# Gate products woven between attention steps in pieces of two blocks, with branches placed anew

## The chip, the cores and the metric

The kernel runs on one core of one Trainium2 chip. The metric is the device time of one execution in microseconds, the median of several runs. Lower is better.

## The reference, cut to what matters

The model has two layers of a mixer with four branches, and after them two hybrid layers that the change does not touch. In f32, with D = 1024, for 512 latent positions, and in the first layer also for 256 context positions:

```python
h = rms_norm(x) * (1 + scale) + shift
y_f = fourier_mix(u_f)                                # branch 0, 3 tiles of 128
o_d = rms_norm(diff_attention(dq, dk, dv, lam)) * gain # branch 1, 4 heads of 128
o_g = gqa_attention(gq, gk, gv)                       # branch 2, 8 heads of 64
y_c = conformer_conv(u_c)                             # branch 3, 3 tiles of 128
g = sigmoid(h @ w_gate)                               # 4 x 1024 columns
merged = g_f * (y_f @ w_f) + g_d * (o_d @ w_d) + g_g * (o_g @ w_g) + g_c * (y_c @ w_c)
out = merged @ w_out
```

Both attentions are softmax over all keys (latent and context, 768 in the latent stages, 256 in the context stage); the differential one subtracts lam times a second softmax.

## The kernel before, in words

**Layout.** Activations lie with features on partitions and positions along the row: NT = 512 positions in a latent stage, 256 in the context stage. Weights come as one stream of blocks of 128 x 128; eight blocks are a chunk of 512 KB (`Weights`). SyncE loads chunks in four slots; ScalarE rounds a chunk to fp32r (`split_hi`, L347), VectorE computes the rest (`split_lo`, L355), two chunks ahead of TensorE, and TensorE multiplies each block in three products, hi x hi, hi x lo and lo x hi (`multiply`, L369 to L371). Each block needs 3 x NT columns.

**Three stages** hold what is changed: the context stage of layer 0, and a latent stage in each layer (`attend_and_merge_stage`, then `merge_last_branch`). Each has eight attention groups (`PairedAttention`): four differential heads, then four pairs of GQA heads. A group has nq = NT / 128 steps, a step is 128 queries with two lanes. In step s, in four micro-steps, TensorE does the scores of s (L991) and, for step s-1, the transposes of the weights (L1023) in one to three fills of one PSUM bank, which ScalarE copies out (L1044); once a group has finished, also its value products (L1005). VectorE finds the negative row maximum of s (L1069), ScalarE does the exponentials of both lanes (L1053), VectorE the reciprocal and the scaling (L1080 to L1093). The score banks are single: the scores of s wait for the exponentials of s-1. The output of a differential head goes out through VectorE (L1074), that of a GQA pair as a hi half through ScalarE (L1059) into `y_hi` and a lo half through VectorE (L1099).

**Gate work** (`Gates`) is a list of tiles: a logit tile is eight blocks (h times 128 gate columns) and ends in a ScalarE tanh (L1192) into one of four gate buffers; a projection tile is three or four blocks (branch output times its weight) and ends in a VectorE product with the gate (L1214), and a sum for all but branch 0 (L1219). Tiles alternate between two PSUM banks. `GATE_PARTS` cuts the list in three: branches 0 and 3 (176 blocks), branch 1 (96 blocks), branch 2 (96 blocks). `gate_part(branches, ahead)` orders the tiles, with logits `ahead` projections ahead.

**The order of the work.** Engines take their instructions in program order, and this order is written by `weave` (L897), which merges generators: each has a list of costs, and an item is placed at the middle of its share of the total. On TensorE an item of `Gates` is a whole tile. There are three weaves, on TensorE, ScalarE and VectorE alike:

- steps 0 to `sub_at` (18 steps in a latent stage, 10 in the context stage) with part 0;
- the next steps, to `sub_end` (3 and 1), with the first four logits of part 1 and with `SubNorm`, the norm of the differential heads;
- the other steps (13 and 7) with the rest of part 1.

`merge_last_branch` then runs part 2 with no attention beside it, and ScalarE and VectorE also write the merged result as hi and lo (L1196, L1223).

`SubNorm`: ScalarE squares four tiles (L1290), into the first four tiles of `y_hi`, TensorE sums over partitions (L1272), ScalarE takes the root (L1293), VectorE the reciprocal (L1305). For each tile, VectorE then spreads the row over 128 columns (L1312), TensorE transposes it (L1281), VectorE scales the tile (L1315), ScalarE and VectorE split it (L1298, L1318).

## Time and profile before

| | |
|---|---|
| runs (3) | 4542.82, 4539.73, 4541.67 us; median 4541.67 |
| profiled execution, own time | 4542.35 us |
| its span | 4540.6 us |
| mean granted TensorE clock | 0.898 of full speed |
| TensorE products (PE) | 3910.3 us busy, 86% |
| weight loads (PEld, beside the products) | 2901.1 us, 64% |
| VectorE (DVE) | 2083.7 us, 46% |
| ScalarE (ACT) | 1443.2 us, 32% |
| GpSimd (POOL) | 73.4 us, 2% |
| DMA | mean 80 GB/s |

The profile is of one execution. Busy time leaves out waits. The ends of products are modelled, so the distance of their starts says more than their duration. The granted clock of TensorE is given as a share of its full speed: 1.00 is 2.4 GHz, 0.50 is 1.2 GHz, and numbers between them are means over a stretch that had both. In the rows, a name such as L1044 is a line of the kernel before, "A <- B" is an engine that stood idle before A until B was done, and x gives a count.

### The profile page before, as it was taken

Reading aid. Unit: us, or ns where it says so; the run is one execution under the profiler, and the core shown is the slowest. Engines: PE = TensorE matmul, PEld = TensorE weight load, DVE = VectorE, ACT = ScalarE, POOL = GpSimd, SP = SyncE. Lnnn points to the kernel's source line nnn. Section 1 sums busy time; section 2 is a strip of 40 time slices with the busy share of each in tenths; the row PEclk is TensorE's granted clock in tenths of the full one; section 3 lists DMA queues with packets and bytes.
Section 4 is the critical chain, followed back from the end, with each engine's and each line's share of the span. In section 5 each row is a group of like instructions: output and inputs, shape, how many; then the busy total and the mean of one; then the engine's idle time right before and its main releaser. Section 6 shows DMA issues by size and latency. Waiting matters only on the chain. (4 is left out here: it accounts for less than half of the span.)

```text
span 4540.6 us, 47186 instructions
## 1 busy us (share of the span) xinstructions
PE 3910.3 (86%) x17646; PEld 2901.1 (64%) x17646; DVE 2083.7 (46%) x3305; ACT 1443.2 (32%) x2501; POOL 73.4 (2%) x62
## 2 busy tenths in 40 slices
PE   8899797989889799788989888799699877898777
PEld 4788796656657688556656656688586434685435
DVE  0755665655433544314655433544423344333363
ACT  0454333234433222123234432222223233223332
POOL 0000000000000000000000000000000010000010
PEclk9999898999999899898999999899798578896688
DMA  7334342211113122352211112122121000220001
GB/s 275 126 116 140 116 165 95 79 47 61 42 34 106 56 97 93 124 183 93 79 47 61 42 42 98 62 96 93 59 95 61 1 19 24 70 93 28 14 5 56
DMA packets 95513, 362.04 MB, mean 80 GB/s; under 512 B 10976, under 2 KB 11232, under 8 KB 93792
## 3 DMA queue, kind: packets, MB, share of 16 engines
q1 hardware_dynamic: 95328, 359.52, 23.9%
q8 instruction: 123, 2.02, 0.2%
q14 instruction: 62, 0.51, 0.0%
HBM read 352.13 MB, written 7.34 MB: 79 GB/s over the span
## 5 line engine op out<-in xcount | busy, mean ns | idle before, releaser
L369 PE MATMUL banks<-h_hi,w_hi 128*128 128x512 f32 (+1 forms) x2808 | 1041.4, 371 | 113.2 <-PEq L566 39.5
L355 DVE TENSOR_TENSOR w_lo<-w_raw,w_hi 128x1024 fp32r<-128x1024 f32 x543 | 663.9, 1223 | 959.9 <-ACT w_hi L347 959.3
L370 PE MATMUL banks<-h_lo,w_hi 128*128 128x512 f32 (+1 forms) x2808 | 1029.0, 366 | 0.0
L371 PE MATMUL banks<-h_hi,w_lo 128*128 128x512 f32 (+1 forms) x2808 | 1027.9, 366 | 0.0
L347 ACT ACTIVATE w_hi<-w_raw 128x1024 fp32r<-128x1024 f32 x543 | 571.7, 1054 | 471.8 <-DMA w_raw<-in_stream 435.9
L369 PEld LDWEIGHTS banks<-h_hi,w_hi 128*128 128x128 f32 x2808 | 538.8, 192 | 216.5 <-issue 121.8
L371 PEld LDWEIGHTS banks<-h_hi,w_lo 128*128 128x128 f32 x2808 | 537.5, 191 | 91.4
L370 PEld LDWEIGHTS banks<-h_lo,w_hi 128*128 128x128 f32 x2808 | 538.9, 192 | 88.4
L369 PE MATMUL banks<-mid_hi,w_hi 128*128 128x512 f32 (+1 forms) x768 | 278.0, 362 | 8.6 <-DVE mid_lo L876 8.6
L370 PE MATMUL banks<-mid_lo,w_hi 128*128 128x512 f32 (+1 forms) x768 | 277.3, 361 | 0.0
L371 PE MATMUL banks<-mid_hi,w_lo 128*128 128x512 f32 (+1 forms) x768 | 277.1, 361 | 0.0
L1069 DVE TENSOR_REDUCE neg_max<-banks 128x2 f32<-128x1536 f32 (+1 forms) x80 | 123.3, 1541 | 104.4 <-PE banks L991 103.9
L1044 ACT ACTIVATE turned<-banks 128x512 f32<-128x512 f32 (+1 forms) x176 | 96.6, 549 | 233.6 <-PE banks L1023 233.4
L855 ACT ACTIVATE mid_hi<-mid 128x512 fp32r<-128x512 f32 (+1 forms) x96 | 53.8, 561 | 360.2 <-DVE mid L873 360.2
L369 PEld LDWEIGHTS banks<-mid_hi,w_hi 128*128 128x128 f32 x768 | 147.6, 192 | 32.4 <-DVE mid_lo L876 9.4
L882 DVE TENSOR_TENSOR y<-y,banks 128x512 f32<-128x512 f32 (+1 forms) x96 | 57.4, 598 | 235.1 <-PE banks L371 235.0
L1023 PE MATMUL banks<-consts,weights 128*128 128x128 f32 x624 | 107.9, 293 | 63.4 <-ACT turned L1044 60.8
L370 PEld LDWEIGHTS banks<-mid_lo,w_hi 128*128 128x128 f32 x768 | 147.8, 192 | 22.9
L371 PEld LDWEIGHTS banks<-mid_hi,w_lo 128*128 128x128 f32 x768 | 147.6, 192 | 23.0
L1859 DVE SCALAR_TENSOR_TENSOR branch<-conv_in,vectors,branch 128x512 f32<-128x512 f32 (+1 forms) x270 | 159.7, 656 | 0.0
L1023 PEld LDWEIGHTS banks<-consts,weights 128*128 128x128 f32 x624 | 74.6, 147 | 102.8 <-ACT turned L1044 75.1
L1053 ACT ACTIVATE weights<-banks,neg_max 128x768 f32<-128x768 f32 (+1 forms) x160 | 129.0, 815 | 25.9 <-DVE neg_max L1069 25.8
(275 smaller groups left out, 5053.9 us busy)
## 6 DMA issues: line engine op xcount, KB each, us to landing
w_raw<-in_stream SPq DMA_DIRECT2D x591, 512.0 KB, 3.5
w_whole<-in_stream SPq DMA_DIRECT2D x48, 512.0 KB, 4.5
x_kept<-x SPq DMA_DIRECT2D x2, 2048.0 KB, 7.2
dft_table<-in_dft SPq DMA_DIRECT2D x2, 2048.0 KB, 7.9
x<-x_kept SPq DMA_DIRECT2D x2, 2048.0 KB, 8.4
x<-in_x SPq DMA_DIRECT2D x1, 2048.0 KB, 11.6
out_x<-x SPq DMA_DIRECT2D x1, 2048.0 KB, 6.3
context<-in_ctx SPq DMA_DIRECT2D x1, 1024.0 KB, 4.9
```

The lines of the kernel that those rows point to most:

```text
L347: self.nc.scalar.activation(self.hi[:, c], self.raw[:, c], ACT.Copy).then_inc(self.hi_ready, 1)
L355: self.nc.vector.tensor_tensor(self.lo[:, c], self.raw[:, c], self.hi[:, c].bitcast(F32), ALU.subtract)\
L369: self.nc.tensor.matmul(out, w_hi, x_hi, start=start, stop=False)
L370: self.nc.tensor.matmul(out, w_hi, x_lo, start=False, stop=False)
L371: mm = self.nc.tensor.matmul(out, w_lo, x_hi, start=False, stop=stop)
L855: nc.scalar.activation(mid_hi[:, t], m[:, t % 2], ACT.Copy).then_inc(mid_hi_ready.sem, 1)
L882: nc.vector.tensor_tensor(y[:, f, 0:NT], y[:, f, 0:NT], K.ps[:, 2 + f % 2, 0:NT], ALU.add)\
L1023: mm = nc.tensor.transpose(K.ps[:, 4, at:at + P], self.weight_at(s - 1, lane)[:, kt * P:(kt + 1) * P], K.const("ident"))
L1044: nc.scalar.activation(self.T[:, lane:lane + lanes, a:b, i * P:(i + 1) * P], K.ps[:, 4, 0:lanes * (b - a) * P].rearrange("p (l k n) -> p l ...
L1053: nc.scalar.activation(self.weight_at(s, lane), self.scores_at(lane, 0, self.n_keys), ACT.Exp, bias=self.nm[:, s % 4, c], accum_out=self.r ...
L1069: nc.vector.reduce_max(self.nm[:, s % 4], scores, AX_X, negate=True).then_inc(self.negmax.sem, 1)
L1859: nc.vector.scalar_tensor_tensor(out=out[:, t], in0=src, scalar=w[:, j * CONV_T + t:j * CONV_T + t + 1], in1=out[:, t], op0=ALU.mult, op1= ...
```

## The change

The list of gate tiles is cut anew. Part 0 is branch 0 alone (88 blocks). Part 1 is branch 3, branch 1 and the first three logits of branch 2 (88 + 96 + 24 = 208 blocks). Part 2 is the rest of branch 2 (72 blocks). The branch 3 tiles thus lie beside the GQA heads and the norm.

On TensorE an item of `Gates` is now a piece of two blocks (or one, at the end of a projection of three). Threads give `weave` the places of their items instead of costs: pieces at their middles; on ScalarE and VectorE each tile has two items, the splits at the tile's start and the evacuation at its end.

Four tiles of `y_hi` are free for the norm while branch 3 waits, so branch 3 moves from `y_hi` tiles 3 to 5 to tiles 4 to 6, and the GQA outputs go to tiles 7, 4, 5, 6 in this order. ScalarE waits for the last branch 3 projection before it writes the outputs of the second to the fourth pair.

In `SubNorm` the spreading copy, its buffer and its semaphore go. TensorE multiplies the reciprocal column, broadcast along its free dimension as the stationary operand, by the identity.

```diff
-GATE_PARTS = [gate_part((0, 3), 1), gate_part((1,), 4), gate_part((2,), 1)]
+LAST = gate_part((2,), 3)
+GATE_PARTS = [gate_part((0,), 2), gate_part((3,), 2) + gate_part((1,), 4) + LAST[:3], LAST[3:]]
+GQA_SLOT = (7, 4, 5, 6)
...
-    at = []
-    for n, (_, costs) in enumerate(threads):
-        total, done = sum(costs), 0.0
-        for c in costs:
-            at.append(((done + c / 2) / total, n))
-            done += c
+    at = [(mark, n) for n, (_, marks) in enumerate(threads) for mark in marks]
     for _, n in sorted(at):
         next(threads[n][0])
+
+
+def even_marks(n):
+    return [(i + 0.5) / n for i in range(n)]
...
+                        self.y_free(act, g)
...
+    def pieces(self, tile):
+        count = KD if tile[0] == "logit" else BRANCH_K[tile[2]]
+        return [range(k, min(k + 2, count)) for k in range(0, count, 2)]
+
+    def marks(self, tiles):
+
+
+        pe, side, at = [], [], 0
+        for tile in tiles:
+            side.append(at)
+            for ks in self.pieces(tile):
+                pe.append(at + len(ks) / 2)
+                at += len(ks)
+            side.append(at)
+        return [m / at for m in pe], [m / at for m in side]
...
-            for k in range(count):
-                if kind == "logit":
-                    hi, lo = self.h_hi[:, k, 0:NT], self.h_lo[:, k, 0:NT]
-                else:
-                    if f == 0:
-                        ready = self.y[n].ready(k)
-                        pe.wait_ge(ready[0], ready[1])
-                    hi, lo = self.y[n].hi(k), self.y[n].lo(k)
-                mm = W.multiply(pe, K.ps[:, 6 + t % 2, 0:NT], self.ends.first[t] + k, hi, lo, k == 0, k == count - 1)
-            if not self.ends.by_chunk[t]:
-                mm.then_inc(self.tile_done.sem, 1)
-            yield
+            for ks in self.pieces(tile):
+                for k in ks:
+                    if kind == "logit":
+                        hi, lo = self.h_hi[:, k, 0:NT], self.h_lo[:, k, 0:NT]
+                    else:
+                        if f == 0:
+                            ready = self.y[n].ready(k)
+                            pe.wait_ge(ready[0], ready[1])
+                        hi, lo = self.y[n].hi(k), self.y[n].lo(k)
+                    mm = W.multiply(pe, K.ps[:, 6 + t % 2, 0:NT], self.ends.first[t] + k, hi, lo, k == 0, k == count - 1)
+                if ks[-1] == count - 1 and not self.ends.by_chunk[t]:
+                    mm.then_inc(self.tile_done.sem, 1)
+                yield
...
             for c in W.splits_for(self.ends.first[t], self.ends.last[t] + 1):
                 W.split_hi(act, c)
+            yield
             if kind == "logit":
...
-            pe.wait_ge(self.wide.sem, self.wide.at(n + 1))
-            if n > 0:
+            if n == 0:
+                pe.wait_ge(self.inverse.sem, self.inverse.at(1))
+            else:
                 pe.wait_ge(self.scaled.sem, self.scaled.at(n))
             for i in range(nt):
-                mm = nc.tensor.transpose(K.ps[:, 5, i * P:(i + 1) * P], self.spread[:, i], K.const("ident"))
+                c = n * nt + i
+                mm = nc.tensor.matmul(K.ps[:, 5, i * P:(i + 1) * P], self.rs[:, c:c + 1].to_broadcast([P, P]),
+                                      K.const("ident"), start=True, stop=True)
...
-            if n == 0:
-                dve.wait_ge(self.inverse.sem, self.inverse.at(1))
-            else:
-                dve.wait_ge(self.summed.sem, self.summed.at(1 + n))
-            nc.vector.tensor_copy(self.spread[:], self.rs[:, n * nt:(n + 1) * nt].unsqueeze(2).to_broadcast([P, nt, P]))\
-                .then_inc(self.wide.sem, 1)
...
-    early = [0, 1, 2, 11, 12, 13]
+    early = [(0, 0), (1, 1), (2, 2), (4, 11), (5, 12), (6, 13)]
...
-        att = PairedAttention(K, scope, groups, NT, n_keys, lam[:, 3:4], lambda g: y_hi[:, 4 + g - n_diff],
+        att = PairedAttention(K, scope, groups, NT, n_keys, lam[:, 3:4], lambda g: y_hi[:, GQA_SLOT[g - n_diff]],
...
-                   Operand(lambda k: y_hi[:, 3 + k], lambda k: y_lo[:, 11 + k], early_ready(3))]
+                   Operand(lambda k: y_hi[:, 4 + k], lambda k: y_lo[:, 11 + k], early_ready(3))]
+        conv_end = gates.tiles.index(("proj", KD - 1, 3))
+        att.y_free = lambda act, g: gates.wait_tile(act, conv_end) if g > n_diff else None
...
-        c1 = gates.costs(1)
-        cut = max(4, len(c1) * (sub_end - sub_at) // (end - sub_at))
-        early_parts = (att.costs(0, sub_at), gates.costs(0))
-        middle = (att.costs(sub_at, sub_end), c1[:cut], sub.costs())
-        late = (att.costs(sub_end, end), c1[cut:])
+        part = GATE_PARTS[1]
+        cut = len(part) * (sub_end - sub_at) // (end - sub_at)
+        assert all(n == 3 for _, _, n in part[:cut])
+        early_at, middle_at, late_at = att.marks(0, sub_at), att.marks(sub_at, sub_end), att.marks(sub_end, end)
+        first_pe, first_side = gates.marks(GATE_PARTS[0])
+        middle_pe, middle_side = gates.marks(part[:cut])
+        late_pe, late_side = gates.marks(part[cut:])
...
             attend, gate = att.pe(pe, 0, end), gates.pe(pe, 1)
-            weave(*zip((attend, gates.pe(pe, 0)), early_parts))
-            weave(*zip((attend, gate, sub.pe(pe)), middle))
-            weave(*zip((attend, gate), late))
+            weave((attend, early_at), (gates.pe(pe, 0), first_pe))
+            weave((attend, middle_at), (gate, middle_pe), (sub.pe(pe), sub.marks()))
+            weave((attend, late_at), (gate, late_pe))
...
             attend, gate = att.act(act, 0, end), gates.act(act, 1)
-            weave(*zip((attend, gates.act(act, 0)), early_parts))
-            weave(*zip((attend, gate, sub.act(act, lambda e: gates.wait_tile(e, gates.part_ends[0] - 1))), middle))
-            weave(*zip((attend, gate), late))
+            weave((attend, early_at), (gates.act(act, 0), first_side))
+            first_done = lambda e: gates.wait_tile(e, gates.part_ends[0] - 1)
+            weave((attend, middle_at), (gate, middle_side), (sub.act(act, first_done), sub.marks()))
+            weave((attend, late_at), (gate, late_side))
```

Between the places shown, the lists handed to `SubNorm` and the VectorE weave change in the same way, and `gates.y[2]` reads the new tiles.

## Rows read from the trace of the kernel before

**Rows 1.** whole span, head of the page
```profile
span 4540.6 us, 47186 instructions
```

**Rows 2.** windows, layer 1: stretch, length, PE, PEld, DVE, ACT, POOL, clock, DMA, GB/s
```profile
2323.20:2519.50 196.30, 188.12 (x832) 130.78 (x834) 110.34 (x144) 82.78 (x153) 0.00 (x0) 1.00 0.17 57
2519.50:2703.70 184.20, 151.99 (x724) 101.76 (x720) 77.98 (x102) 75.82 (x137) 0.00 (x0) 0.93 0.11 36
2703.70:2774.00 70.30, 67.08 (x288) 54.15 (x288) 30.81 (x36) 21.34 (x28) 0.00 (x0) 1.00 0.28 93
```

**Rows 3.** windows of layer 0's latent stage and the context stage, same columns
```profile
964.60:1419.00 454.40, 410.55 (x1840) 288.54 (x1840) 219.29 (x281) 179.97 (x316) 0.00 (x0) 0.96 0.16 54
...
245.20:425.00 179.80, 164.91 (x1288) 151.92 (x1288) 113.21 (x209) 93.05 (x188) 0.00 (x0) 0.98 0.41 135
```

**Rows 4.** waits (us, times, longest), layer 1: 2323.2 to 2519.5; 2583 to 2703.7
```profile
ACT gate L1192 <- PE banks L371: 47.5, 15, 5.7
...
PE banks L1023 <- ACT turned L1044: 18.8, 17, 2.4
```

**Rows 5.** windows of 4 us in layer 1's stage, columns as above
```profile
2540.00:2544.00 4.00, 0.66 (x4) 0.42 (x4) 1.58 (x4) 3.54 (x8) 0.00 (x0) 0.83 0.27 103
2544.00:2548.00 4.00, 3.18 (x12) 2.89 (x13) 2.10 (x4) 1.24 (x3) 0.00 (x0) 0.50 0.02 4
...
2628.00:2632.00 4.00, 2.29 (x12) 1.49 (x14) 1.76 (x4) 2.91 (x7) 0.00 (x0) 0.93 0.00 0
2632.00:2636.00 4.00, 4.00 (x17) 2.62 (x14) 1.76 (x1) 1.26 (x2) 0.00 (x0) 0.65 0.01 2
2592.00:2596.00 4.00, 3.31 (x21) 2.25 (x20) 1.76 (x1) 1.99 (x5) 0.00 (x0) 1.00 0.00 0
```

**Rows 6.** timeline of TensorE: the first products of two successive blocks
```profile
2607.89 0.39 PE L369 MATMUL banks<-h_hi,w_hi 128*128 128x512 f32 x1
...
2608.59 0.39 PE L369 MATMUL banks<-h_hi,w_hi 128*128 128x512 f32 x1
```

**Rows 7.** groups of instructions by form, 2323.2 to 2519.5
```profile
L1053 ACT ACTIVATE weights<-banks,neg_max 128x768 f32<-128x768 f32 x36 | 32.1, 902 | 6.4 <-DVE neg_max L1069 6.4
L1069 DVE TENSOR_REDUCE neg_max<-banks 128x2 f32<-128x1536 f32 x18 | 31.6, 1755 | 20.5 <-PE banks L991 20.3
L355 DVE TENSOR_TENSOR w_lo<-w_raw,w_hi 128x1024 fp32r<-128x1024 f32 x22 | 26.9, 1221 | 18.5 <-ACT w_hi L347 18.5
...
L1089 DVE SCALAR_TENSOR_TENSOR weights<-weights,row_sum 128x768 f32<-128x768 f32 x16 | 16.3, 1019 | 0.6
...
L1044 ACT ACTIVATE turned<-banks 128x512 f32<-128x512 f32 x19 | 11.3, 597 | 58.4 <-PE banks L1023 58.4
L1087 DVE TENSOR_SCALAR weights<-weights,row_inverse 128x768 f32<-128x768 f32 x16 | 9.8, 614 | 0.0
...
L1053 ACT ACTIVATION_READ_ACCUMULATOR weights<-banks,neg_max 128x1 f32 x36 | 7.3, 204 | 0.0
...
L1080 DVE RECIPROCAL row_inverse<-row_sum 128x2 f32<-128x2 f32 x18 | 2.9, 163 | 24.2 <-ACT weights L1053 24.2
```

**Rows 8.** groups of instructions by form, 2703.7 to 2774
```profile
L1214 DVE SCALAR_TENSOR_TENSOR gated<-gate,banks 128x512 f32<-128x512 f32 x8 | 5.5, 688 | 16.3 <-PE banks L371 16.3
```

**Rows 9.** timeline of VectorE: the maxima of two successive steps
```profile
2592.91 1.76 DVE L1069 TENSOR_REDUCE neg_max<-banks 128x2 f32<-128x1536 f32 x1 [2.78 <-PE banks L991]
...
2599.54 1.76 DVE L1069 TENSOR_REDUCE neg_max<-banks 128x2 f32<-128x1536 f32 x1 [0.25 <-PE banks L991]
```

**Rows 10.** timeline of TensorE: a differential head's value products, then four transposes
```profile
2417.02 3.70 PE L1005 MATMUL banks<-turned,v_latent 128*128 128x512 f32 x8
2420.56 1.88 PE L1005 MATMUL banks<-turned,v_context 128*128 128x512 f32 x4
2422.27 0.60 PE L1023 MATMUL banks<-consts,weights 128*128 128x128 f32 x4
```

**Rows 11.** groups of instructions by form, 2519.5 to 2583
```profile
L1312 DVE COPY gated<-sub_rstd 128x512 f32<-128x512 f32 x4 | 1.7, 419 | 0.0
```

More of the change, by code:

```diff
@@ L958, in __init__, with marks @@
         self.flat = K.ps[:, 0:2 * self.wide // BANK, :].rearrange("p b n -> p (b n)")
-    def costs(self, first, last):
-        return [1.0] * (self.MICRO * (last - first))
+    def marks(self, first, last):
+        return even_marks(self.MICRO * (last - first))
     def scores_at(self, lane, a, b):
@@ L1206, in dve @@
                 W.split_lo(dve, c)
+            yield
             if kind == "proj":
@@ L1259, in __init__, with marks @@
         self.rs = K.sb(scope, "sub_rstd", [n * self.nt])
-    def costs(self):
-        return [1.0, 1.0] + [1.0] * len(self.tiles)
+    def marks(self):
+        return even_marks(2 + len(self.tiles))
     def pe(self, pe):
@@ L1387, in _ @@
             attend, gate = att.dve(dve, 0, end), gates.dve(dve, 1)
[L1388 to L1392 removed]
+            weave((attend, early_at), (gates.dve(dve, 0), first_side))
+            weave((attend, middle_at), (gate, middle_side), (sub.dve(dve), sub.marks()))
+            weave((attend, late_at), (gate, late_side))
+    gates.y[2] = Operand(lambda k: y_hi[:, GQA_SLOT[k]], lambda k: y_lo[:, 7 + k],
                          lambda k, sem=att.out_done.sem, v=att.out_done.at(n_diff): (sem, v + k + 1))
```

25 lines of the change are left out of this document (9 added, 16 removed).

## Prediction

> **What bounds the kernel now.** I read the busy shares first, then the three attention stages by stretch, then their waits, then the clock. The span is 4540.6 us [rows 1]; the change touches only the three stages that run attention and gate products together, so I cut those out. In the latent stage of layer 1 (450.8 us), TensorE is busy 188.1 of 196.3 us while the differential heads run, 152.0 of 184.2 us from there to the end of the attention, and 67.1 of 70.3 us in the last branch, which runs alone [rows 2]. No other engine comes near: VectorE, the next, is busy 110.3, 78.0 and 30.8 us of them. So TensorE bounds these stages, and what can be won is its idle time and its slow time. The layer 0 latent stage takes 454.4 us with 410.6 busy, the context stage 179.8 with 164.9 [rows 3].
>
> Busy time times granted clock gives the work at full clock: 188.1 + 152.0 x 0.93 + 67.1 = 396.6 us, so layer 1's stage loses 54 us. It loses 8 in the first stretch, 43 in the second (32 idle, 11 slow), 3 in the last.
>
> The waits say how. In the last 121 us of the second stretch a transpose of weights waits 17 times, 18.8 us in all, for ScalarE to empty the single transpose bank, because nothing stands between two fills; in the first, ScalarE stands 15 times (47.5 us) in front of an eight-block tile that TensorE has not finished [rows 4]. The idle time costs twice: from 2540 TensorE is busy 0.66 of 4 us and then runs at clock 0.50, that is at 1.2 GHz instead of 2.4; at 2628 it is busy 2.29 of 4 us and the next 4 us are granted 0.65. At 2592, with 3.31 of 4 busy, it stays at 1.00 [rows 5].
>
> **What moves.** A block is three products; at full clock blocks start 0.70 us apart [rows 6]. Before, the first stretch carries 176 blocks (branches 0 and 3: 16 logit tiles of 8, 16 projections of 3), the second 96 (8 x 8 + 8 x 4), the lone branch 96. After: 88, then 88 + 96 + 24 = 208, then 72. No product is dropped, the total is 368 both times. I work on layer 1 and use it for both latent stages.
>
> **First stretch, now bound by attention's chain.** Attention's own work there is 188.1 - 176 x 0.70 = 64.9 us. With 88 blocks TensorE has 126.5 us in 18 steps, 7.0 each. But a step also has a chain that one score buffer forces. From the end of the exponentials of a step: VectorE normalises (0.16, 0.61 and 1.02), takes the next maximum 1.76, ScalarE does two lanes of 0.90 + 0.20 [rows 7]. That is 5.75; with some 0.5 for the hand-overs (an estimate: the floor of two rows further on leaves no more) 6.3 us. VectorE also gets 11 splits of 1.22 [rows 7] and 8 gate products of 0.69 [rows 8] in 18 steps, 1.05 a step; about half falls into its slack behind the maximum: 6.8 us. The shortest steps of before, 2592.91 to 2599.54, take 6.63 [rows 9], so I trust that size. Four of the 18 steps also hold a head's value products, 5.25 us [rows 10]. Without those, TensorE has (64.9 - 4 x 5.25) / 18 = 2.4 us of scores and transposes a step and 3.4 of gates, 5.8, so in 14 steps the chain decides: 14 x 6.8 = 95. In the other four TensorE needs 11.05, with a hand-over 11.2: 45. Sum 140 us against 196.3. TensorE idles some 13 us here, 5 more than before: the price of taking half the filler out.
>
> **Second stretch, now bound by TensorE.** Its attention work is 152.0 x 0.93 - 96 x 0.70 = 74.2 us. 208 blocks add 145.6: 219.8. Pieces of two blocks (1.4 us) put 2.2 to 2.4 us between any two attention steps on TensorE, where a hand-over is one ScalarE copy of 0.60 [rows 7] and 0.3 of latency, so the 18.8 us go; the exponentials (2.2) and maximum (1.76) of a step stand against 12 to 14 us of TensorE per step. What stays late is the norm between the two kinds of head, where four squares and two table loads of ScalarE sit ahead of exponentials. I take 5.5 us idle, a sixth of the 32 there now, most of it at that norm, and no slow clock: 225.3 against 184.2. Bounds: 0 idle, or all of the 43 as before.
>
> **Last branch.** 96 - 72 = 24 blocks less, 16.8 us: 53.5 against 70.3. The order now ends in three projections in a row. VectorE needs for each three operations of 0.69 and a wait of 0.7 for ScalarE [rows 8], some 2.9 us, and a split of 1.22 comes among them, while TensorE gives it one per 2.8 us. The end comes 1.2 us later than before: 54.7.
>
> **Small edits.** The four spread copies (0.42 each [rows 11]) and their semaphore go: they are on the path only where TensorE waits at the norm, inside the 5.5. The conv branch's wait in front of heads 1 to 3 costs nothing: its last projection is at 0.29 of the last 13 steps on TensorE, and ScalarE asks at 0.36; if it were late, exponentials queue behind it and TensorE waits. DMA moves the same chunks in another order, at 36 to 93 GB/s in these stretches [rows 2], and no engine is seen short of it there. Sixteen transposes per latent stage become plain products. Four transposes record 0.60 us, so at most 0.15 each; a plain f32 product of 512 columns takes 3.54 / 8 = 0.44, so 0.11 for 128 columns [rows 10]. Between nothing and 0.15 x 16 = 2.4 us, I take nothing. The Trainium skill (TensorE: Matmul & The Clock Gate, Terms) says transposes of f32 run four times faster than plain ones. By that rule each of the sixteen would cost 3 x 0.15 more, 7 us a latent stage and 4 in the context's half-size one, for 4490; the row of the value products speaks against it.
>
> **Sum.** 140 + 225.3 + 54.7 = 420.0 against 450.8: 30.8 saved; layer 0's stage should take the same, 454.4 - 420.0 = 34.4. Context: 164.9 x 0.98 = 161.6 of work, 18.2 lost [rows 3]. Its steps have a chain of half the length, but the splits of VectorE stay at 1.22 and its edges stay, so I let it lose 13: 5 saved. Together 70 us. The profiled execution took 4542.35 us, 0.7 above the median of 4541.67; 4542.35 - 70 = 4472.
>
> **Rivals.**
> A, the clock. TensorE idles about 1 us in each of the 14 steps, and the first stretch may run partly at 1.2 GHz for it. For: at 2628 it idled 1.7 of 4 us and the clock fell behind that. Against: at 2592 it idled 0.7 of 4 and kept 1.00 [rows 5], and the stretch to come idles 13 of 140 in all. The slow stretch at 2544 cost 3.18 x 0.50 = 1.6 us; one in each second step makes 9 x 1.6 = 14 per latent stage, of which I let 2 fall into the chain's slack: 4472 + 24 = 4496. The Trainium skill (same page, A second HAM failure mode: psum-queue depth-cycling) says that frequent short idling between product groups alone makes the clock swing. By that rule this case would hold; the rows agree with it only where TensorE idled longer. Chance 0.18.
> B, the second stretch is not filled. Copies 2 and 3 of a step stand behind the exponentials in ScalarE's queue, as do the gate tiles' own waits; if TensorE still finds them late, the idle 32.2 us stays in place of 5.5: 27 per latent stage, 4472 + 54 = 4526. Against: 2.3 us of filler against 0.9. Chance 0.12.
> C, slower. The first stretch does not shrink with its work. Its steps take 196.3 / 18 = 10.9 us now; if ScalarE, in front of a gate tile whose pieces are now spread over a step and a half, holds back the exponentials queued behind it, they stay there: 56 us per latent stage, 4472 + 112 = 4584. It decides from 140 / 18 + 70 / 36 = 9.7 us a step. For: 47.5 us of such waits [rows 4]. Against: a tile's evacuation is now placed at the tile's end, no longer at its middle. Chance 0.05.
> D, the pieces weave but what is won is lost at other places, within 0.2% of before: 0.03.
>
> **Numbers.** The forecast has 0.62: 4452 to 4492, with each first-stretch step 0.3 us off on either side (11 us over both stages), the second stretch 0 to 11 idle (11), and context at 0 to 10 saved. The range 4440 to 4512 takes in A and half of the way to B. About 9 us (0.2%) is what a measurement of this kernel can tell. The forecast is the likeliest case, so 4472 stands. Faster 0.92 (forecast, A, B), same 0.03, slower 0.05.
>
> **What would show it.** Right: first stretch near 140 us, VectorE's maxima 6.5 to 7 us apart there in three steps of four; second stretch near 225 us with clock 1.00 and hardly a wait of a transpose for its copy; last branch near 54. Rival A: clock below 0.97 in the first stretch. B: the waits for the transpose copy above 10 us. C: maxima over 9.7 us apart. The forecast falls if the second stretch takes more than 245 us or the first more than 160.

## The result, and the profile after

The changed kernel takes 4471.53 us (median of 4 runs, 4465.75 to 4474.63) against 4540.70 us for the kernel before (4 runs): the ratio is 0.9848, with a 95% interval of 0.9831 to 0.9865. The forecast was 4472. The profiled execution of the changed kernel took 4474.63 us.

Line numbers shift by a few in the changed kernel: scores are L992 (before L991), value products L1006, transposes L1024 (L1023), the copy of a transpose L1045 (L1044), exponentials L1054 (L1053), the maximum L1071 (L1069), VectorE's scaling L1089 and L1091 (L1087 and L1089), the gate tanh L1209 (L1192), the norm row L1301 (L1281), rounding a chunk L349 (L347). Kernels with an added line shift them by one more.

The head of the page of the changed kernel, which answers to [rows 1]:

```profile
span 4472.9 us, 47254 instructions
...
PE 3894.6 (87%) x17686; PEld 2892.1 (65%) x17686; DVE 2079.0 (46%) x3293; ACT 1441.4 (32%) x2501; POOL 73.3 (2%) x62
```

TensorE has the same work less some slow time, and the span is 67.7 us shorter. The stretches show where. First the three of layer 1's stage, cut at the same events as [rows 2], then the whole latent stage of layer 0 and the context stage, as [rows 3]; columns as there:

```profile
2293.20:2432.60 139.40, 127.18 (x568) 81.06 (x569) 87.02 (x117) 68.41 (x134) 0.00 (x0) 1.00 0.12 38
2432.60:2649.90 217.30, 216.18 (x1066) 156.20 (x1065) 103.02 (x127) 93.33 (x160) 0.00 (x0) 0.99 0.20 63
2649.90:2707.60 57.70, 52.26 (x225) 41.83 (x223) 27.26 (x33) 17.28 (x23) 0.00 (x0) 1.00 0.30 91
...
972.20:1388.70 416.50, 398.17 (x1856) 280.61 (x1856) 217.41 (x277) 179.00 (x316) 0.00 (x0) 0.99 0.19 59
...
247.40:433.50 186.10, 168.97 (x1296) 155.62 (x1296) 112.91 (x205) 93.10 (x188) 0.00 (x0) 0.97 0.41 131
```

Layer 1's stage takes 414.4 us instead of 450.8, layer 0's 416.5 instead of 454.4; the context stage takes 186.1 instead of 179.8. That is 36.4 + 37.9 - 6.3 = 68.0 us of the 67.7. The first stretch has idle time (12.2 us), the second has next to none (1.1 us, with 32 before), and its clock is 0.99 instead of 0.93.

Waits of the first stretch of layer 1's stage (us in all, times, longest):

```profile
ACT turned L1045 <- PE banks L1024: 60.3, 18, 8.6
PE banks L992 <- ACT weights L1054: 5.5, 4, 3.2
PE banks L1024 <- ACT turned L1045: 5.2, 7, 1.1
PE banks L1024 <- DVE weights L1091: 1.4, 3, 0.7
```

And of the norm's steps, 2432.6 to 2493:

```profile
PE banks L371 <- ACT gate L1209: 0.9, 1, 0.9
PE banks L1024 <- ACT turned L1045: 0.2, 1, 0.2
```

The second stretch has no wait of weight left: behind the norm, where [rows 4] had 18.8 us of waits of a transpose for its copy, TensorE now has none. In the first stretch ScalarE stands for TensorE's transposes far longer than TensorE for ScalarE. TensorE's own 12.2 us are 5.5 for exponentials (of these 3.2 once, at the start of the stage), 5.2 in seven waits for a copy, and 1.4 for VectorE's scaling.

The wait of 3.2 us at the start comes in both latent stages, 3.16 us in layer 0 and 3.17 in layer 1. Windows of 4 us around it, first layer 0, then layer 1:

```profile
976.00:980.00 4.00, 2.14 (x10) 1.39 (x8) 3.34 (x3) 2.26 (x3) 0.00 (x0) 1.00 0.00 0
980.00:984.00 4.00, 2.70 (x8) 1.19 (x8) 1.88 (x4) 1.25 (x4) 0.00 (x0) 0.51 0.00 0
...
2298.00:2302.00 4.00, 1.21 (x6) 0.65 (x4) 2.42 (x2) 2.27 (x4) 0.00 (x0) 1.00 0.00 0
2302.00:2306.00 4.00, 3.20 (x17) 2.13 (x18) 3.54 (x5) 0.93 (x3) 0.00 (x0) 1.00 0.00 0
```

In layer 0 the clock fell to 0.51 behind it and was 0.64 in the next 4 us; in layer 1 it stayed at 1.00. TensorE's waits in the two first stretches are otherwise almost the same, so this one fall is most of the 2.1 us between them (141.5 and 139.4 us). So a difference of some 2 us between single stretches of two kernels can come from this alone.

### The profile page after: what moved, and what is told of

The parts are those of the page before. It is cut to its first block and busy times, and to the rows that moved or that the text cites. A ratio compares the mean times of both kernels' runs of the same rounds, so it can differ in the third digit from the quotient of the medians.

```text
span 4472.9 us, 47254 instructions
## 1 busy us (share of the span) xinstructions
PE 3894.6 (87%) x17686; PEld 2892.1 (65%) x17686; DVE 2079.0 (46%) x3293; ACT 1441.4 (32%) x2501; POOL 73.3 (2%) x62
## 5 line engine op out<-in xcount | busy, mean ns | idle before, releaser
L349 ACT ACTIVATE w_hi<-w_raw 128x1024 fp32r<-128x1024 f32 x543 | 571.4, 1054 | 483.8 <-DMA w_raw<-in_stream 459.7
L1045 ACT ACTIVATE turned<-banks 128x512 f32<-128x512 f32 (+1 forms) x176 | 96.6, 549 | 283.2 <-PE banks L1024 283.1
L1071 DVE TENSOR_REDUCE neg_max<-banks 128x2 f32<-128x1536 f32 (+1 forms) x80 | 123.3, 1541 | 46.5 <-PE banks L992 46.0
L1699 DVE TENSOR_REDUCE row_max<-banks 128x1 f32<-128x256 f32 (+3 forms) x128 | 56.5, 441 | 169.4 <-PE banks L1580 169.4
L1054 ACT ACTIVATE weights<-banks,neg_max 128x768 f32<-128x768 f32 (+1 forms) x160 | 128.7, 814 | 20.0 <-DVE neg_max L1071 19.5
L608 PE MATMUL banks<-consts,squares 128*128 128x1 f32 x248 | 49.6, 328 | 96.9 <-ACT squares L585 96.9
```

Source lines behind the costliest of these rows:

```text
L349: self.nc.scalar.activation(self.hi[:, c], self.raw[:, c], ACT.Copy).then_inc(self.hi_ready, 1)
L1045: nc.scalar.activation(self.T[:, lane:lane + lanes, a:b, i * P:(i + 1) * P], K.ps[:, 4, 0:lanes * (b - a) * P].rearrange("p (l k n) -> p l ...
L1054: nc.scalar.activation(self.weight_at(s, lane), self.scores_at(lane, 0, self.n_keys), ACT.Exp, bias=self.nm[:, s % 4, c], accum_out=self.r ...
L1071: nc.vector.reduce_max(self.nm[:, s % 4], scores, AX_X, negate=True).then_inc(self.negmax.sem, 1)
L1699: nc.vector.reduce_max(mx[:, c], scores_at(m, c0, c1), AX_X).then_inc(row_max.sem, 1)
```

## The experiments

The first four ask what earns the time: the pieces, the new cut, or the norm row.

### Whole tiles in the new cut

```diff
     def pieces(self, tile):
-        return [range(k, min(k + 2, count)) for k in range(0, count, 2)]
+        return [range(count)]
```

> The changed kernel, but with a gate tile again as one item on TensorE (the new cut of the parts, the places of splits and evacuations and the norm stay). Theory P, the pieces: they alone fill the hand-overs of attention, so the second stretch of a latent stage, 217 us in the changed kernel, comes back with idle time of 15 us or more, the waits of a transpose for its copy with it, and the time is 4505 to 4530 us. Theory C, the cut: 208 blocks beside the GQA heads instead of 96 are filler enough in any portion; the second stretch stays under 224 us and the time under 4485.

Measured: 4552.83 us, ratio 1.0029 (1.0017 to 1.0042). Stretches of layer 1's stage, and a wait of its second stretch:

```profile
2331.10:2490.80 159.70, 135.13 (x573) 85.36 (x573) 87.16 (x117) 68.82 (x135) 0.00 (x0) 0.96 0.11 35
2490.80:2726.40 235.60, 220.00 (x1050) 159.41 (x1051) 102.52 (x127) 92.80 (x160) 0.00 (x0) 0.97 0.18 58
2726.40:2786.60 60.20, 54.75 (x235) 43.79 (x234) 27.26 (x34) 17.28 (x23) 0.00 (x0) 1.00 0.28 88
...
PE banks L1024 <- ACT turned L1045: 15.6, 14, 2.9
```

The second stretch has 15.6 us idle, all of it waits of transposes for their copy, and the clock is 0.97 instead of 0.99. P holds and C falls. P was too narrow, though, and its 4505 to 4530 us too low: the first stretch also grew, from 139.4 to 159.7 us, with 24.6 idle and a clock of 0.96. Without pieces the new cut is slower than the kernel before, although this kernel has the new norm row too. It also keeps the new places of splits and evacuations, so against the changed kernel only the pieces differ, and against the kernel before the cut, the places and the norm row.

### Pieces in the old cut

```diff
-GATE_PARTS = [gate_part((0,), 2), gate_part((3,), 2) + gate_part((1,), 4) + LAST[:3], LAST[3:]]
+GATE_PARTS = [gate_part((0, 3), 1), gate_part((1,), 4), gate_part((2,), 1)]
...
-        cut = len(part) * (sub_end - sub_at) // (end - sub_at)
+        cut = max(4, len(part) * (sub_end - sub_at) // (end - sub_at))
```

> The changed kernel, but with the parts of before (branches 0 and 3, branch 1, branch 2 alone; 176, 96 and 96 blocks). Theory P: pieces fill the second stretch also with 96 blocks. Its work at full clock is 74.2 + 67.2 = 141.4 us, with 6 idle 148, the first stretch takes 190 and the last 70.5, together 408 per latent stage against 414 in the changed kernel: 4452 to 4465 us. Theory C: with 96 blocks the chain of maximum and exponentials shows, the second stretch stays above 170 us and the time above 4510.

Measured: 4478.16 us, ratio 0.9862 (0.9845 to 0.9878). Stretches of layer 1's stage:

```profile
2286.00:2475.50 189.50, 187.50 (x833) 130.13 (x834) 110.55 (x144) 83.33 (x153) 0.00 (x0) 1.00 0.19 59
2475.50:2635.30 159.80, 145.01 (x731) 95.69 (x730) 74.81 (x96) 74.14 (x136) 0.00 (x0) 0.97 0.13 40
2635.30:2708.80 73.50, 68.64 (x295) 55.09 (x293) 32.32 (x38) 21.32 (x28) 0.00 (x0) 1.00 0.30 93
```

C is wrong; P has the side right and the gain too large: the second stretch came to 159.8, not 148, with 14.8 us idle. 96 blocks do not hide all of attention's hand-overs there, and 208 do. But the first stretch idles only 2 us with 176 blocks, where it idles 12 with the changed kernel's 88. The new cut gains 422.8 - 414.4 = 8 us in layer 1's stage and 6 in layer 0's, and gives 5.6 back in the context stage (180.5 against 186.1). The intervals of the two kernels overlap: the re-placing of the branches is the smallest part of the change.

### 38 blocks back in the first stretch

```diff
+CONV = gate_part((3,), 2)
+GATE_PARTS = [gate_part((0,), 2) + CONV[:6], CONV[6:] + gate_part((1,), 4) + LAST[:3], LAST[3:]]
```

> The changed kernel with the first six tiles of branch 3 (38 blocks) moved from the second stretch back to the first, so that 126 blocks stand beside the differential heads and 170 beside the rest. If the first stretch is bound by attention's chain (139.4 us with 12 idle), it takes in 26.6 us of work for 16 to 19 us: 156 to 158, while the second falls by 26 to 191; a latent stage gains 8 to 10 us and the time is 4450 to 4458. If the 12 idle us come from something that each gate piece brings along, the first stretch grows by the whole 26.6 or more, and the time stays at 4468 to 4476.

Measured: 4454.98 us, ratio 0.9812 (0.9796 to 0.9828). The first two stretches of layer 1's stage:

```profile
2275.80:2435.20 159.40, 154.49 (x688) 102.36 (x690) 95.60 (x126) 74.96 (x143) 0.00 (x0) 1.00 0.16 50
2435.20:2629.40 194.20, 190.39 (x948) 134.84 (x945) 93.73 (x118) 86.00 (x151) 0.00 (x0) 0.98 0.19 57
```

The first stretch took in 26.6 us of products for 20.0 us, the second gave back 23. The stage is 411.4 us long. So there was room in the first stretch, less than I had said (16 to 19 us were expected): idle fell from 12.2 to 4.9. This kernel is faster than both; against the changed one it gains 16.5 us. The time lies in the forecast, but not for its reason: layer 1's stage gained 3.0 us and layer 0's 4.5 (411.9 against 416.4), not 8 to 10 each, and the context stage, of which the forecast said nothing, gained 7.4 (178.7 against 186.1). What the cut does there was not looked into by a run of its own.

### The old norm row in the changed kernel

```diff
-                mm = nc.tensor.matmul(K.ps[:, 5, i * P:(i + 1) * P], self.rs[:, c:c + 1].to_broadcast([P, P]),
-                                      K.const("ident"), start=True, stop=True)
+                mm = nc.tensor.transpose(K.ps[:, 5, i * P:(i + 1) * P], self.spread[:, i], K.const("ident"))
...
+            nc.vector.tensor_copy(self.spread[:], self.rs[:, n * nt:(n + 1) * nt].unsqueeze(2).to_broadcast([P, nt, P]))\
+                .then_inc(self.wide.sem, 1)
```

The waits of before come with it; the spread row lies in a free tile of `y_hi`.

> The changed kernel with the norm row of before: VectorE spreads the row over 128 columns and TensorE transposes it. The forecast's account: the copies of 0.42 us lie beside TensorE's gate work, and a plain product costs no more than a transpose, so nothing changes beyond 3 us: 4469 to 4475. Rival: the norm is on the path, each of the four copies and its two hand-overs (about 0.7 us) is paid in all three stages, 8 us or more: over 4479. By the Trainium skill's rule that f32 transposes are four times faster than plain products, this kernel would be faster than the changed one, by 18 us if all sixteen of a latent stage are on the path.

Measured: 4495.21 us, ratio 0.9900 (0.9883 to 0.9916), so 23.7 us more than the changed kernel. My account is wrong and the rival right. The second stretch of layer 1's stage, and a wait in it:

```profile
2441.70:2668.50 226.80, 219.13 (x1049) 157.04 (x1048) 104.47 (x131) 93.57 (x160) 0.00 (x0) 0.97 0.20 61
...
PE banks L1300 <- DVE sub_squares L1331: 6.8, 4, 3.5
```

The stretch is 226.8 us instead of 217.3: 6.5 us more idle, and 3.0 more busy at a clock of 0.97 instead of 0.99. Four waits of TensorE for the copy make 6.8 us. VectorE's timeline shows why a copy of 0.42 us costs up to 3.5:

```profile
2472.37 1.23 DVE L357 TENSOR_TENSOR w_lo<-w_raw,w_hi 128x1024 fp32r<-128x1024 f32 x1 [0.65 <-ACT w_hi L349]
...
2473.71 1.15 DVE L1095 TENSOR_SCALAR weights<-weights,row_inverse 128x768 f32<-128x768 f32 x2
2474.77 0.42 DVE L1331 COPY sub_squares<-sub_rstd 128x512 f32<-128x512 f32 x1
```

TensorE's timeline, the products that wait for it:

```profile
2475.25 1.12 PE L1300 MATMUL banks<-consts,sub_squares 128*128 128x128 f32 x4 [3.49 <-DVE sub_squares L1331]
```

And windows of 4 us around them:

```profile
2472.00:2476.00 4.00, 0.75 (x4) 0.76 (x5) 2.78 (x5) 0.82 (x2) 0.00 (x0) 0.74 0.00 0
2476.00:2480.00 4.00, 4.00 (x13) 3.33 (x12) 1.44 (x2) 1.11 (x2) 0.00 (x0) 0.50 0.08 14
```

The copy stands in VectorE's queue behind a step's scaling, this needs the step's exponentials and stands behind the split of a chunk, and the split had waited 0.65 us for ScalarE's rounding. TensorE idled 3.49 us, and the window of 4 us behind it ran at clock 0.50, that is 1.2 GHz. The broadcast product needs the reciprocal only, which is there long before, and the scaling of the tile before. What the new norm row takes away is thus not a copy of 0.42 us but TensorE's dependence on a place in VectorE's queue.

The same two kernels settle the price of the products. In the changed kernel, four plain products of 128 columns:

```profile
2452.66 1.05 PE L1301 MATMUL banks<-consts,sub_rstd 128*128 128x128 f32 x8
```

In this one, four transposes:

```profile
2464.17 0.66 PE L1300 MATMUL banks<-consts,sub_squares 128*128 128x128 f32 x4 [0.61 <-DVE sub_squares L1331]
```

Four plain ones take 1.05 us and are recorded as eight, four transposes 0.66. That is 0.4 us more for four, so 1.6 us a latent stage, inside the 0 to 2.4 of the forecast. From the first of the four to the next product on TensorE it is 0.81 us (2452.66 to 2453.47) against 0.42 (2464.17 to 2464.59), the same difference. The Trainium skill (TensorE: Matmul & The Clock Gate, Terms) puts transposes of f32 at four times the speed; here a plain product takes 1.6 times as long by duration and 1.9 times by the starts, and the kernel with transposes is the slower one.

### Each half alone, on the kernel before

The norm row alone, in the kernel before (VectorE's copy and its semaphore go with it):

```diff
-                mm = nc.tensor.transpose(K.ps[:, 5, i * P:(i + 1) * P], self.spread[:, i], K.const("ident"))
+                mm = nc.tensor.matmul(K.ps[:, 5, i * P:(i + 1) * P], self.rs[:, c:c + 1].to_broadcast([P, P]),
+                                      K.const("ident"), start=True, stop=True)
```

> The kernel before with one part of the change alone, the norm row as a broadcast product. Theory N, that TensorE stands at the norm for VectorE's spread copy, which is queued behind a step's maximum and scaling: the part works here too, where TensorE waits 5.0 us for the copies in layer 1's stage and goes slow after two of them: 5 to 9 us per latent stage and 2 to 4 in the context stage less, 4518 to 4529. Rival, that the copies are hidden in lumps of eight blocks and only hurt between small pieces: within 4 us of before.

And the pieces alone with their new places, which is the changed kernel with two of the edits above, the old parts and the old norm row:

```diff
-GATE_PARTS = [gate_part((0,), 2), gate_part((3,), 2) + gate_part((1,), 4) + LAST[:3], LAST[3:]]
+GATE_PARTS = [gate_part((0, 3), 1), gate_part((1,), 4), gate_part((2,), 1)]
...
+                mm = nc.tensor.transpose(K.ps[:, 5, i * P:(i + 1) * P], self.spread[:, i], K.const("ident"))
```

> The kernel before with the other half: pieces of two blocks with their new places for splits and evacuations, but the parts and the norm row of before. If the parts of the change add up, this is the run with the old cut (4478) plus what the old norm row cost beside the new cut (23.7 us): 4498 to 4505. If the norm costs less beside logit tiles alone than beside the conv tiles, 4484 to 4495. Above 4520 the pieces would not be the larger half.

Measured: the norm row alone 4525.51 us, ratio 0.9969 (0.9959 to 0.9980); the pieces alone 4507.78 us, ratio 0.9933 (0.9916 to 0.9949). With the norm row alone, layer 1's second stretch is

```profile
2506.00:2685.80 179.80, 151.78 (x740) 101.71 (x736) 76.43 (x98) 75.79 (x137) 0.00 (x0) 0.94 0.12 37
```

4.4 us shorter than in [rows 2], and the context stage 4.2 us shorter than in [rows 3] (175.6). The whole latent stages gained 2.7 us (layer 1, whose last branch took 1.6 longer) and 5.9 (layer 0), against 5 to 9 expected; the time is in the forecast. Theory N holds also among lumps, with the size at its lower edge. With the pieces alone, the first two stretches of layer 1's stage and the context stage are

```profile
2312.70:2502.20 189.50, 187.52 (x833) 130.11 (x834) 110.56 (x144) 83.34 (x153) 0.00 (x0) 1.00 0.18 59
2502.20:2669.30 167.10, 143.43 (x715) 93.43 (x714) 76.55 (x100) 74.44 (x136) 0.00 (x0) 0.96 0.13 38
...
248.70:440.00 191.30, 168.63 (x1288) 155.04 (x1288) 113.96 (x209) 93.00 (x188) 0.00 (x0) 0.96 0.41 127
```

The first stretch gains 6.8 us and the second 17.1, but the last branch loses 4.8 (75.1 us) and the context stage 11.5. 4507.78 lies just above the first forecast's 4498 to 4505. The parts do not add up: the norm row alone gives 14 us and the pieces alone 32, but the kernel with both 62. With pieces the norm row is worth 29.6 us (4507.78 to 4478.16), twice as much as with lumps. In one table, medians in us ("pieces" come with the new places of splits and evacuations; the whole tiles of the old cut have the old places, those of the new cut the new ones):

| | old norm row | new norm row |
|---|---|---|
| old cut, whole tiles | 4540.7 (before) | 4525.5 |
| old cut, pieces | 4507.8 | 4478.2 |
| new cut, whole tiles | not run | 4552.8 |
| new cut, pieces | 4495.2 | 4471.5 (the change) |

So in the new cut pieces by themselves are worth 81 us. In the old cut the 32 us are those of pieces and places together; no run has the one without the other.

### Is the first stretch bound by VectorE's chain?

```diff
-                    nc.vector.tensor_scalar(w[0], w[0], ri[:, 0:1], None, ALU.mult).then_inc(self.scaled.sem, 1)
+                    half = self.n_keys // 2
+                    nc.vector.tensor_scalar(w[0][:, 0:half], w[0][:, 0:half], ri[:, 0:1], None, ALU.mult).then_inc(self.scaled.sem, 1)
```

and likewise the subtraction behind it.

> The changed kernel with VectorE's scaling and subtraction of the differential heads' weights done on the first 384 of 768 keys (128 of 256 in the context stage); the other half stays unscaled, so this kernel computes something else. That takes some 0.8 us out of each step's chain of VectorE and ScalarE and nothing from TensorE. Chain theory: the first stretch of a latent stage falls from 139.4 to 128 to 133 us (TensorE's own work of 126.5 is the floor), the second stays, and the time is 4450 to 4460. If TensorE's 12 idle us there have another cause (the transpose copy on ScalarE, the gate tiles), the first stretch stays above 136 and the time above 4466.

Measured: 4466.68 us, ratio 0.9839 (0.9823 to 0.9856). The first stretch of layer 1's stage:

```profile
2290.30:2429.00 138.70, 128.46 (x568) 81.63 (x569) 78.03 (x117) 68.39 (x134) 0.00 (x0) 0.99 0.12 38
```

138.7 us against 139.4, where 128 to 133 was expected, with VectorE 9 us less busy. The chain theory falls, and the total is just above the 4466 of its rival. In the changed kernel two maxima of VectorE already stood closer than the 6.8 us that I had worked out as the floor of a step:

```profile
2378.57 1.75 DVE L1071 TENSOR_REDUCE neg_max<-banks 128x2 f32<-128x1536 f32 x1
...
2380.36 0.90 ACT L1054 ACTIVATE weights<-banks,neg_max 128x768 f32<-128x768 f32 x1 [1.14 <-DVE neg_max L1071]
...
2382.03 0.20 ACT L1054 ACTIVATION_READ_ACCUMULATOR weights<-banks,neg_max 128x1 f32 x1
...
2383.19 1.02 DVE L1091 SCALAR_TENSOR_TENSOR weights<-weights,row_sum 128x768 f32<-128x768 f32 x1
...
2384.12 1.75 DVE L1071 TENSOR_REDUCE neg_max<-banks 128x2 f32<-128x1536 f32 x1
```

They are 5.55 us apart, and this comes four times in layer 1's 18 steps (the others lie 6.1 to 9.1 us apart, two with value products between them 11.7 and 13.6). Such a step is the forecast's chain itself, end to end: the maximum, both lanes of exponentials from 2380.36 to 2382.23, and the normalising up to the next maximum. The chain is there, but it takes 5.55 us and not 6.8. The two lanes take 1.87 us and not 2.2, because the record of each accumulator read (0.20) starts before the exponentials ahead of it end. With half the scaling the shortest distance fell only to 5.34 us.

I then thought of TensorE's own order, in which a gate piece can stand between scores and transposes:

```diff
-            weave((attend, early_at), (gates.pe(pe, 0), first_pe))
+            close = [m + (i % 4 == 0) * 0.99 / len(early_at) for i, m in enumerate(early_at)]
+            weave((attend, close), (gates.pe(pe, 0), first_pe))
```

> The changed kernel, but in the first stretch TensorE takes the scores of a step right before the transposes of the step before, so that no gate piece stands between them. Theory O, TensorE's own order: a step lasts as long as scores, the pieces between scores and transposes, transposes, the copy of 0.60 us and the exponentials of 2.2, since ScalarE takes the copy before the exponentials; with 5.55 us as the floor where no piece is between. Then the first stretch of a latent stage falls from 139.4 to 130 to 136 us, with the maxima never under 5.5 us apart and no longer scattered from 5.55 to 9, and the time is 4452 to 4466. Rival, the floor is TensorE's work plus hand-overs that only move: the first stretch stays within 2 us of 139.4 and the time at 4468 to 4475. If instead VectorE's scaling, which the transposes wait for, now shows, the stretch grows by 3 us or more.

Measured: 4466.94 us, ratio 0.9845 (0.9829 to 0.9861). The first stretch of layer 1's stage and two waits in it:

```profile
2286.50:2426.00 139.50, 127.09 (x569) 80.82 (x570) 87.18 (x117) 68.98 (x135) 0.00 (x0) 1.00 0.13 38
...
PE banks L1024 <- ACT turned L1045: 5.2, 7, 1.1
PE banks L1024 <- DVE weights L1091: 1.7, 3, 0.9
```

139.5 us: the rival is right for the stretch, and the maxima still lie 5.55 to 10.45 us apart, two of them further. The total is 4.6 us lower, which is inside the scatter of the runs; most of it is the context stage, where the edit works too, and which took 182.3 us instead of 186.1. So neither edit shortened the stretch. The chain's 5.55 us lie just below the 5.8 us of TensorE's own work, and what idles is what the rows of waits list: hand-overs of a copy, mostly of 0.7 us, where no piece happens to stand, the start of the stage, and a few exponentials. The waits for the copy are 5.2 us in 7 before and after this edit. That TensorE's own work and these short waits set the length is what is left, and agrees with the 38 blocks above, of which the stretch paid 20.0 of 26.6 us; no run removes the waits and shows it.

### The lone last branch, and the context stage

```diff
+GATE_PARTS = [gate_part((0,), 2), gate_part((3,), 2) + gate_part((1,), 4), gate_part((2,), 1)]
```

> The changed kernel with branch 2 whole again behind the attention and its projections one behind each logit tile (184 blocks in the second stretch, 96 in the last). Where the second stretch is bound by TensorE, moving 24 blocks into it gained nothing, and three projections in a row at the end cost some: the second stretch falls by 16.8 us, the last rises by 13 to 16, and the time is 4460 to 4470, a little below the changed kernel. Rival: the three logit tiles beside the attention are part of the gain, because they fill its last steps; then the time is 4480 or more.

Measured: 4474.78 us, ratio 0.9855 (0.9838 to 0.9871). The second and last stretch of layer 1's stage:

```profile
2427.50:2630.80 203.30, 201.04 (x999) 143.53 (x998) 97.87 (x122) 88.86 (x155) 0.00 (x0) 0.99 0.19 60
2630.80:2704.90 74.10, 69.30 (x291) 55.52 (x289) 32.33 (x38) 21.32 (x28) 0.00 (x0) 0.98 0.29 92
```

277.4 us together against 275.0 in the changed kernel. Neither forecast: the second stretch fell by 14.0 us instead of 16.8 and the last rose by 16.4, and the whole stages are 1.4 us (layer 0) and 2.4 us (layer 1) longer. Of the re-placing, this part is next to neutral, as one expects where TensorE is busy on both sides.

The context stage is the one place where the change loses. There ScalarE waits for DMA while copies and exponentials queue behind (us in all, times, longest; changed kernel):

```profile
ACT w_hi L349 <- DMA w_raw<-in_stream: 30.3, 22, 3.0
```

Splits now stand at a tile's start. This run puts them back to the tile's middle and leaves evacuations at the end:

```diff
-            side.append(at)
+            start = at
...
-            side.append(at)
+            side += [(start + at) / 2, at]
```

> The changed kernel, but with a tile's splits placed at the middle of the tile, as before the change, and only its evacuation at the end. Theory L: in the context stage, where a chunk lasts 2.8 us on TensorE, splits at the tile's start find the chunk not yet loaded and ScalarE stands for DMA (30.3 us against 21.7 before the change) with copies and exponentials queued behind. Then that wait falls under 25 us, the context stage from 186 to 180 to 183, and the time to 4464 to 4469. Rival: ScalarE has time to wait there, the context stage stays within 2 us of 186, or TensorE now waits for late splits and it grows.

Measured: 4470.16 us, ratio 0.9852 (0.9835 to 0.9868). The context stage, and the same wait:

```profile
247.00:426.60 179.60, 165.92 (x1296) 153.11 (x1296) 112.24 (x205) 92.67 (x188) 0.00 (x0) 0.99 0.43 135
...
ACT w_hi L349 <- DMA w_raw<-in_stream: 22.8, 18, 2.4
```

The stage and the wait fell as theory L says: 179.6 us and 22.8 us of waits. The time did not follow, 4470.16 is above the 4464 to 4469 expected. The latent stages change by +1.9 (layer 1) and -0.1. The profiled spans differ by 4.8 us, the medians by 1.4, which is inside their scatter. And the wait does not order the stages of different kernels: the pieces in the old cut have 32.3 us of it and a context stage of 180.5, the 38 blocks moved back 30.1 us and 178.7. Late splits shorten this stage; that they do it through the wait for DMA is argued, not shown. Two runs combined this with the cut that had been faster. First whole tiles in the context stage alone, with splits and evacuations at the middle:

```diff
-        return [range(k, min(k + 2, count)) for k in range(0, count, 2)]
+        step = 2 if self.NT == SEQ else count
+        return [range(k, min(k + step, count)) for k in range(0, count, step)]
...
+            side += [start, at] if self.NT == SEQ else [(start + at) / 2] * 2
```

> The kernel with 38 blocks of branch 3 moved back to the first stretch (4455 us), and in the context stage alone whole tiles with splits and evacuations at their middle, as before the change. If pieces of 0.7 us are too fine for that stage, where each brings VectorE and ScalarE work nearer to TensorE's pace, the context stage falls from 178.7 to 172 to 176 us (175.6 is what the kernel before with the new norm row had), with the latent stages at 411: 4449 to 4453. If lumps cost there what they cost in the latent stages, it grows to 183 or more: over 4459.

Measured: 4452.85 us, ratio 0.9814 (0.9797 to 0.9830); the context stage took 177.7 us, 1.0 less than with pieces, between the two forecasts, while the time is in the first. Then late splits there, and pieces everywhere:

```diff
+CONV = gate_part((3,), 2)
+GATE_PARTS = [gate_part((0,), 2) + CONV[:6], CONV[6:] + gate_part((1,), 4) + LAST[:3], LAST[3:]]
...
+            side += [start, at] if self.NT == SEQ else [(start + at) / 2, at]
```

> The fastest cut (38 blocks of branch 3 back in the first stretch, 4455 us), and in the context stage alone the splits at the middle of a tile, evacuations at its end, pieces of two blocks everywhere. Theory L, that early splits make ScalarE stand for DMA in the context stage: late splits took 6.4 us off that stage in the changed kernel, and what is worth 4 to 6 us there should come here too, 172 to 175 us for the context stage against 178.7, with the latent stages at 411 to 412: 4448 to 4452. Rival: the 6.4 us were luck in how that stage's pieces fall and the cut had already won them; then the stage stays above 177 and the time at 4453 to 4457.

Measured: 4450.51 us (5 runs), ratio 0.9801 (0.9788 to 0.9815), the fastest median of the study; its interval overlaps with those of the last kernel and of the 38 blocks alone. Its context stage and the wait:

```profile
247.20:421.70 174.50, 165.16 (x1296) 152.57 (x1296) 112.63 (x205) 92.83 (x188) 0.00 (x0) 0.99 0.45 139
...
ACT w_hi L350 <- DMA w_raw<-in_stream: 18.7, 20, 2.6
```

The stage took 174.5 us where early splits with the same cut took 178.7, and the wait is 18.7 us instead of 30.1. That is inside the first forecast, and the rival, that the cut had already won this, falls. The latent stages took 411.5 and 408.7 us.

## Why the prediction was right or wrong

**The total.** 4472 was forecast and 4471.53 came. That closeness is partly luck: errors of both signs cancel. The latent stages took 416.5 and 414.4 us instead of 420.0, together 9 less, and the context stage 186.1 instead of 174.8, 11 more. With the old norm row the same kernel takes 4495, which is 23 us over the forecast: 5 in each latent stage (425 instead of 420) and 14 in the context stage by the profile. The norm row, which I had priced at nothing, gave the same 24 us back.

**The first stretch** was forecast at 140 us and took 139.4 and 141.5. The size is right, the mechanism is not. "in 14 steps the chain decides" failed: with 0.8 us a step less on VectorE the stretch stays at 138.7. The chain's own length is 5.55 us, not 6.8, and four steps of 18 show it; the sign that I had named, maxima 6.5 to 7 us apart in three steps of four, came once (6.69) among the sixteen distances without the two long ones. I had charged VectorE's splits and gate products half to the chain, and had taken the 6.63 of [rows 9] for a floor although other work stood in that step. TensorE's own 5.8 us and its short hand-overs add up to about the same sum; that the two agree is luck.

**The second stretch** was forecast at 225.3 us and took 217.3, the last at 54.7 and took 57.7, together 280.0 against 275.0. The last is 3 us longer only because the cut between the two lies at VectorE's last output, while TensorE still works on the second stretch's pieces: its first product of the lone part starts at 2653.05. Most of the 5 us is idle time of the second stretch, 1.1 us where 5.5 was forecast. The tail of three projections is as forecast: between the last branch's products and the next stage TensorE idles 5.4 us, with 4.0 before, 1.4 us more for the 1.2 said. That the transposes' waits go and the clock stays up was right: 0.2 us of them are left in the norm's steps and none behind it, and the clock is 0.99.

**The small edits** hold the step that failed most. "they are on the path only where TensorE waits at the norm, inside the 5.5" priced the norm row at nothing. It is worth 23.7 us: 8.5 and 10.6 in the latent stages and 3.3 in the context stage by their profiles. With the old row the second stretch takes 226.8 us, close to the forecast of 225.3, which had in effect been made for a kernel without this part. I had counted the copy's duration and not its place in VectorE's queue. The price of the plain products rested on a misreading of [rows 10]: the 3.54 us with x8 are four products, each recorded twice, so 0.88 us for 512 columns and 0.22 for 128, not 0.44 and 0.11. Measured between starts it is 0.20. At 0.4 us for four this error is small, and read rightly the row still speaks against the factor of four, only less strongly.

**Context** was forecast 5 us faster and is 6.3 slower. The words "the splits of VectorE stay at 1.22 and its edges stay" named the right engine work, but the sum took no account of where the new marks put the splits: at the tile's start, where the chunk has often not landed. Late splits give 6.5 us of that stage back. Against the 175.6 us of the kernel before with the new norm row alone the stage is 10.5 us longer, so some 4 us of the loss are left, and where they come from stays open.

**The rivals.** A, the clock, did not come in the way feared: the first stretch ran at 1.00 and 0.98 with 12 us idle, the second at 0.99. The Trainium skill (TensorE: Matmul & The Clock Gate, A second HAM failure mode: psum-queue depth-cycling) expects short idling between groups to make the clock swing. Here the many short waits, mostly of 0.7 us, did not. The one long wait of 3.2 us brought the clock down in layer 0's stage and not in layer 1's; 24.6 us idle, in the whole-tile kernel, went with 0.96. B did not come with pieces and did with whole tiles in the same cut (15.6 us of such waits). C: with whole tiles the first stretch did stay long (159.7 us), though far below 196. That evacuations moved to the tile's end was given there as a reason against C, and was not tested by itself.

## What to carry to other kernels

Price a removed instruction by what its consumer waits for, in its engine's queue, not by its duration: twelve copies, four in each of three stages, were worth 24 us. Fine pieces pay where an engine hands work to another many times a step, and here the more so once a fixed dependence between them was gone; moving work from one stretch bound by an engine to another gained next to nothing. Where the fill is uneven, try to share it: 126 and 170 blocks beat both 88 and 208 and 176 and 96, though half of that gain came in the context stage and is not explained. And compare each stage with its forecast, not the total alone: the totals of the change and of the 38 blocks lay in their forecasts while their stages did not.

## What the runs showed of the hardware that I had not expected

- A plain f32 product of 128 columns is recorded as two and takes 1.05 us for four, against 0.66 for four transposes; to the next product it is 0.81 against 0.42.
- After 3.49 us idle TensorE ran at clock 0.50 in the next window of 4 us. Idle times of mostly 0.7 us, seven in 139 us, left the clock at 1.00.
- Waits of 3.16 and 3.17 us at the same place of the same kernel had different ends: 0.51 behind the one, 1.00 behind the other.
- Two exponentials of 768 elements with their accumulator reads, recorded with 0.90 and 0.20 us each, took 1.87 us together.
